# Gated-recurrence and softmax mixer: heads by pairs, four weight units held back into the softmax steps

## The reference, cut to what matters

```python
def _hybrid_mixer(h, w_in, conv_w, conv_b, gate_w, gate_b, lam, f_b, qk_g, w_out):
    u, gate, q, k, v, f = jnp.split(h @ w_in, ...)
    y_rnn = _rglru_branch(u, gate, ...)            # convolution, two gates, a scan over the tokens, gelu(gate)
    qh = _rmsnorm(_heads(q, 8), qk_g[0]); kh = _rmsnorm(_heads(k, 8), qk_g[1])
    logf = jax.nn.log_sigmoid(f + f_b)
    # softmax attention, 8 heads of 64, causal:
    # s = q.k * scale + c[query] - c[key],  c = cumsum(logf);  p = softmax(s);  y = p @ v
    return jnp.concatenate([y_rnn, y_fox], axis=-1) @ w_out
```

## Time and profile before

| | us |
|---|---|
| median of 3 runs | 2993.77 |
| the profiled execution | 2994.8 |
| its span, first to last instruction | 2993.1 |
| TensorE busy | 2903.7 (97%) |
| TensorE weight loads | 2344.5 (78%) |
| VectorE busy | 1471.6 (49%) |
| ScalarE busy | 1001.0 (33%) |
| mean granted TensorE clock | 0.988 of full speed |

### The profile page before, as it was taken

One profiled execution on the slowest core, in us unless ns is written; L12 is line 12 of the kernel. 1 busy time (PEld: TensorE's weight loads), 2 busy tenths in 40 slices (PEclk: granted clock), 3 DMA queues, 4 the chain that ended last, 5 costly groups with the idle time before them and its releaser, 6 DMA issues. The chain is left out here.

```text
span 2993.1 us, 33982 instructions
## 1 busy us (share of the span) xinstructions
PE 2903.7 (97%) x13410; PEld 2344.5 (78%) x13410; DVE 1471.6 (49%) x1906; ACT 1001.0 (33%) x1128; POOL 32.8 (1%) x66
## 2 busy tenths in 40 slices
PE   7999999999999999999999999999999989899998
PEld 5888887568888888888887888888866567688886
DVE  5764346446753476543544444436444843533333
ACT  4222227333222322223544322325432443232222
POOL 0000000000000000000000000000000000000000
PEclk9999999899999999999999999999999999999999
DMA  4432231014432343223111322234211112122221
GB/s 165 140 119 98 100 127 71 15 64 141 146 107 107 108 142 133 105 99 101 60 54 57 113 98 98 89 109 155 102 55 53 43 56 98 72 99 98 94 103 71
DMA packets 63742, 289.03 MB, mean 97 GB/s; under 512 B 9392, under 2 KB 26160, under 8 KB 33568
## 3 DMA queue, kind: packets, MB, share of 16 engines
q1 hardware_dynamic: 55072, 257.97, 24.3%
q0 software_dynamic: 8000, 29.50, 2.9%
q10 hardware_dynamic: 576, 0.23, 0.0%
HBM read 285.57 MB, written 2.10 MB: 96 GB/s over the span
## 5 line engine op out<-in xcount | busy, mean ns | idle before, releaser
L912 DVE TENSOR_TENSOR sb_WL<-sb_RAW,sb_WH 128x2048 fp32r<-128x2048 f32 x243 | 556.8, 2292 | 852.9 <-ACT sb_WH L403 852.9
L1602 PE MATMUL PS<-sb_HH,sb_WH 128*128 128x512 f32 x2352 | 934.2, 397 | 32.9 <-DVE sb_WL L912 24.2
L1603 PE MATMUL PS<-sb_HL,sb_WH 128*128 128x512 f32 x2352 | 920.1, 391 | 0.0
L1604 PE MATMUL PS<-sb_HH,sb_WL 128*128 128x512 f32 x2352 | 919.9, 391 | 0.0
L403 ACT ACTIVATE sb_WH<-sb_RAW 128x2048 fp32r<-128x2048 f32 x243 | 464.9, 1913 | 797.6 <-PE PS L1604 794.8
L1602 PEld LDWEIGHTS PS<-sb_HH,sb_WH 128*128 128x128 f32 x2352 | 444.8, 189 | 137.6 <-issue 38.6
L1603 PEld LDWEIGHTS PS<-sb_HL,sb_WH 128*128 128x128 f32 x2352 | 444.6, 189 | 95.2 <-issue 5.0
L1604 PEld LDWEIGHTS PS<-sb_HH,sb_WL 128*128 128x128 f32 x2352 | 444.2, 189 | 94.4
L1602 PE MATMUL PS<-ff_GH,sb_WH 128*128 128x512 f32 x880 | 342.4, 389 | 1.9 <-DVE sb_WL L912 1.9
L1604 PE MATMUL PS<-ff_GH,sb_WL 128*128 128x512 f32 x880 | 342.3, 389 | 0.0
L1603 PE MATMUL PS<-ff_GL,sb_WH 128*128 128x512 f32 x880 | 342.3, 389 | 0.0
(11 more groups left out here) (341 smaller groups left out, 2674.8 us busy)
## 6 DMA issues: line engine op xcount, KB each, us to landing
sb_RAW<-in_weights SPq DMA_DIRECT2D x233, 1024.0 KB, 4.8
ff_ADAW<-in_w_ada POOLq DMA_DIRECT2D x48, 512.0 KB, 4.0
sb_RAW<-in_weights SPq DMA_DIRECT2D x16, 512.0 KB, 4.9
sb_XT<-in_x SPq DMA_DIRECT2D x1, 2048.0 KB, 9.9
out_t<-sb_XT SPq DMA_DIRECT2D x4, 512.0 KB, 3.2
b_CT<-in_ctx POOLq DMA_DIRECT2D x1, 1024.0 KB, 5.4
sb_RAW<-in_weights SPq DMA_DIRECT2D x4, 256.0 KB, 4.1
hy_BD<-in_c_gates POOLq DMA_DIRECT2D x1, 512.0 KB, 3.5
```

The source lines that it names most:

```text
L912: dve.tensor_tensor(WL[slot][:, :], RAW[slot][:, :], f32(WH[slot][:, :]), ALU.subtract).then_inc(*T["w_lo"].up())
L1602: pe.matmul(out, wh, xh, start=start, stop=False)
L1603: pe.matmul(out, wh, xl, start=False, stop=False)
L1604: return pe.matmul(out, wl, xh, start=False, stop=stop)
```

## The change

The first mixer is laid out like the second one, with these parts:

1. Units: seven are run before the attention, in the order u, u, f, q0, k0, gate, gate (q0 and k0 hold the first four heads' pairs, two each). The second half of q and k, and all of v, are held back: q2 and k2 come in one slot from two half loads (`load_pair`), then v0, then q3 and k3, then v1. They are run as eight `part_step`s of half a unit, in bank 7.
2. Heads by pairs: for every row block, the q.k matmuls of both heads stand side by side, one on rows 0 to 63, one on rows 64 to 127. The order of the blocks is 2, 0, 1, 3, packed in three banks per head. A pair's `values` alternate likewise on the lower and the upper 64 output partitions of bank 6.
3. `CH` holds the high part of c in rows 0 to 7 and the low part in rows 32 to 39, and `SEL` has its selection rows twice, so one matmul adds both.
4. `turned(h)`: the ten transposes go back into the head's own score banks, one ScalarE copy of 1280 columns takes them out (`fox_pt`).
5. The normalisation of q and k is split into eight single steps (`squares`, `head_sum`, `root`, `normed`), the last four between the steps of the attention; the forget gate's chain is moved to the start. The recurrence (`recur`), its gelu and its product stand between softmax steps.
6. The first output group's matmuls (`first_out`) are put around the last pair's values; the other three groups are written out instead of looped, with banks (7,0), (4,5), (6,7), (4,5).

```diff
-HY_VISITS = ([("feat", (n, i)) for n in ("u", "q", "k", "gate") for i in range(2)] + [("gates", ("f", 0))]
-             + [("tok", ("v", i)) for i in range(2)])
+HY_VISITS = [("feat", ("u", 0)), ("feat", ("u", 1)), ("gates", ("f", 0)), ("feat", ("q", 0)), ("feat", ("k", 0)),
+             ("feat", ("gate", 0)), ("feat", ("gate", 1))]
+HY_UNITS = [0, 1, 8, 2, 4, 6, 7, (3, 5, 0), 9, (3, 5, 1), 10]
+HY_STEPS = [("q", 2), ("k", 2), ("v", 0), ("v", 1), ("q", 3), ("k", 3), ("v", 2), ("v", 3)]
+FOX_OFF = {3: 0, 2: 512, 0: 896, 1: 1024}
+FOX_ORDER = (2, 0, 1, 3)
```

ScalarE's program, from the first four gates on:

```diff
+            gate(0, hy["R"])
+            squares(2)
+            squares(3)
+            logs_table()
+            root(0)
+            root(1)
...
+            prepare(6)
+            root(2)
+            root(3)
...
+            gate(1, hy["I"])
...
+            prepare(7)
+            logs_table()
+            fox_exp(0)
+            fox_exp(1)
+            squares(4)
+            fox_pt(0)
+            fox_pt(1)
+            root(4)
...
+            squares(5)
+            prepare(8)
+            logs_table()
+            fox_exp(2)
+            fox_exp(3)
```

VectorE's program, from the first softmax step on:

```diff
+            fox_max(0)
+            fox_max(1)
+            recur(0)
+            fox_norm(0)
+            fox_norm(1)
+            take_part(0)
+            recur(1)
+            recur(2)
+            recur(3)
+            normed(4)
+            take_part(1)
+            prepare(8)
+            fox_max(2)
+            fox_max(3)
+            fox_norm(2)
+            fox_norm(3)
+            normed(5)
+            take_part(2)
```

TensorE's program:

```diff
+            def fox_scores(p):
+                pe.wait_ge(T["qk_norm"].sem, (3, 4, 6, 8)[p])
+                for i in FOX_ORDER:
+                    o, w = FOX_OFF[i], P * (i + 1)
+                    for h in (2 * p, 2 * p + 1):
+                        r = slice(64 * (h % 2), 64 * (h % 2) + 64)
+                        if p and i == FOX_ORDER[0]:
+                            pe.wait_ge(T["fx_pt"].sem, h - 1)
+                        pe.matmul(zs(h)[:, o:o + w], hy["Q"][r, p, P * i:w], hy["K"][r, p, 0:w], start=i != 0, stop=True, skip_group_check=True)
+                    for h in (2 * p, 2 * p + 1):
+                        pe.matmul(zs(h)[:, o + P * i:o + w], hy["EYE"][:, :], hy["MASK"][:, :], start=False, stop=True, skip_group_check=True)
+                        pe.matmul(zs(h)[:, o:o + w], hy["SEL"][:, h, :], hy["CH"][:, 0:w], start=False, stop=True, skip_group_check=True)\
+                            .then_inc(*T["fx_s"].up())
...
+            visit(0)
+            norm(N_NORM["mix0"])
+            visit(1)
+            visit(2)
+            pe.wait_ge(T["rms_ready"].sem, N_NORM["mix0"] + 1)
+            rms_columns(4)
+            visit(3)
+            visit(4)
...
             gates(0)
+            head_sum(0)
+            head_sum(1)
             visit(5)
+            head_sum(2)
+            head_sum(3)
             gates(1)
             visit(6)
...
             fox_scores(0)
+            part_step(0)
+            turned(0)
+            turned(1)
+            head_sum(4)
+            part_step(1)
+            fox_scores(1)
+            head_sum(5)
+            part_step(2)
+            part_step(3)
+            turned(2)
+            turned(3)
+            fox_values(0)
+            part_step(4)
+            fox_scores(2)
+            head_sum(6)
+            part_step(5)
+            fox_values(1)
+            turned(4)
+            turned(5)
+            head_sum(7)
+            part_step(6)
+            fox_scores(3)
+            part_step(7)
+            turned(6)
+            turned(7)
+            fox_values(2)
...
+            first_out(*hyo, 0, 0, 6)
+            first_out(*hyo, 0, 6, 7)
+            fox_values(3)
+            first_out(*hyo, 1, 0, 7)
+            first_out(*hyo, 0, 7, 8)
+            first_out(*hyo, 1, 7, 8).then_inc(*T["visit_done"].up())
+            residual(RES["hy"], U_HYO, (8,), HY_YH, HY_YL, False, g_from=1)
```

More of the change, by code:

```diff
@@ L261, in raw_need, with pairs_before @@
             return 16 * (u // 2 + 1) + (32 if u % 2 else -32) * (u >= U_SBO)
+        def pairs_before(u):
+            return sum(isinstance(unit, tuple) for unit in HY_UNITS[:u - U_HY + 1])
         def sb_raw(k):
@@ L315, in _ @@
                     load(s, 2 * i + s + 2)
[L316 to L317 removed]
+            for k, unit in enumerate(HY_UNITS):
+                sp.wait_ge(T["w_lo"].sem, U_HY + k - 1)
+                if isinstance(unit, tuple):
+                    load_pair((U_HY + k) % 2, (U_HY + unit[0], U_HY + unit[1]), unit[2])
+                else:
+                    load((U_HY + k) % 2, U_HY + unit)
+            with sp.Fori(0, (U_SB - U_HYO) // 2) as i:
+                for s in range(2):
+                    sp.wait_ge(T["w_lo"].sem, 2 * i + (U_HYO + s - 1))
+                    load((U_HYO + s) % 2, 2 * i + (U_HYO + s))
             for k, (kind, q) in enumerate(SB_LOADS):
@@ L583, in roots @@
[L583 to L595, removed]
+                    act.activation(dst[:, m, :], PS[:, 2 + m, :], ACT.Sigmoid, bias=col("gate_b", 4 * g + m)).then_inc(*T["rg_sig"].up())
@@ new lines, in _ @@
+            take(4)
+            prepare(5)
+            normed(0)
+            normed(1)
+            take(5)
+            prepare(6)
+            normed(2)
+            normed(3)
+            for m in range(4):
+                gain(m)
+            dve.wait_ge(T["xc_ready"].sem, 4)
+            for m in range(4):
+                dve.wait_ge(T["rg_sig"].sem, 4 + m + 1)
+                step(dve.tensor_tensor(I[:, m, :], I[:, m, :], XC[:, m, :], ALU.mult))
+            take(6)
+            prepare(7)
@@ new lines, in _ @@
+            for m in range(4):
+                dve.tensor_tensor(XC[:, m, :], XC[:, m, :], hy["GT"][:, m, :], ALU.mult).then_inc(*T["y_f32"].up())
+            take_part(3)
+            for m in range(4):
+                out_low(m + 1, HY_YH[m], HY_YL[m], XC[:, m, :])
+            prepare(9)
+            fox_low(0)
+            take_part(4)
+            fox_max(4)
+            fox_max(5)
+            fox_norm(4)
+            fox_norm(5)
+            normed(6)
+            take_part(5)
+            fox_low(1)
@@ L1276, in _ @@
+            prepare(10)
+            normed(7)
+            take_part(6)
+            fox_max(6)
+            fox_max(7)
+            fox_norm(6)
+            fox_norm(7)
+            take_part(7)
+            prepare(11)
+            fox_low(2)
+            fox_low(3)
+            residual(RES["hy"], U_HYO, 1, False, 1.0, "ffn1", ahead=U_HYO + 1)
             ffn(1)
@@ L1738, in _, with head_sum @@
-            for k in range(5):
-                if k == 2:
-                    pe.wait_ge(T["rms_ready"].sem, N_NORM["mix0"] + 1)
-                visit(k)
-                if k == 0:
-                    norm(N_NORM["mix0"])
+                    pe.matmul(PS[:, 2 + m, :], hy["BD"][:, 4 * g + m, :], hy["XC"][:, m, :], start=True, stop=True).then_inc(*T["rg_mm"].up())
+            def head_sum(i):
+                pe.wait_ge(T["qk_sq"].sem, i + 1)
+                if i >= 2:
+                    pe.wait_ge(T["qk_rms"].sem, i - 1)
+                pe.matmul(PS[:, i % 2 if i < 4 else 6, :], hy["B64"][:, :], SQT[:, i % 2, :], start=True, stop=True).then_inc(*T["qk_ss"].up())
```

446 lines of the change are left out of this document (211 added, 235 removed).

## The result

The changed kernel takes 2941.58 us (median of four runs, 2941.07 to 2943.32) where the kernel before took 2994.03 beside it (2993.01 to 2995.91): a ratio of 0.9825 [0.9808, 0.9842], 52 us less. The profiled execution is 2943.32 with a span of 2941.6.

A forecast was written before the change was run, and what follows sets the result against it. TensorE, busy 97% of the span, was taken to bound the kernel. Savings of 50.4 less 2.0 for extra changes and 1.1 for waits gave 47.3 off 2994.8, forecast 2947 us, range 2938 to 2961.

The forecast's parts named there:

- Stage and windows: First mixer, from 394 to the end of the fourth output unit: 223 instead of 270 us.
- Scores, 17.8: Attention scores: a pair of heads takes about 6.15 us against 10.60, saving 17.8 over four pairs.
- rival D: Array halves do not overlap with mask and c matmuls between blocks; 17.7 comes back, 2965; chance 3%.
- Values, 9.2: Attention values: four pairs at 2.3 us instead of eight heads, saving 9.2.
- Transposes, 8.5: Attention transposes: ten in a row take 1.3 us instead of 2.36 per head, saving 8.5.
- Clock and waits: Around the attention: low clock 8.0, waits 2.8 before first scores, 1.7 before output, 1.7 in heads, 0.7 idle, all saved.
- first head's waits: Attention: first and last head have 1.7 us more of waits than the steady ones, which go.
- Extra changes, -2.0: Around half units and single head sums: some ten more fp32/fp32r changes on TensorE at 0.2 each, costing 2.0 us.
- Waits, -1.1: New TensorE waits in the attention: 0.2 us at `head_sum(4)` and 0.9 at `part_step(3)`, costing 1.1.
- rival B: Softmax chain on the other engines replaces the old waits, 2.5 us late per pair: 2957; chance 24%.
- rival F: ScalarE table switches each take as long again as their load, 1.28 us more: 2953; chance 4%.
- Rival C and E: C: one long wait takes the clock down, 2958, 8%. E: finely cut stretch holds TensorE at low clock, 3052, 3%.

The follow-up runs named there:

- one_c: The kernel before with one c matmul per score block instead of two, low part of c in eight more rows: 3001.20 us, ratio 1.0006.
- rows_apart: The changed kernel with each head's mask and c matmuls directly behind its q.k, so the two heads' q.k are not side by side: 2977.35 us, ratio 0.9933.
- cols_apart: The changed kernel with a pair's values done one head after the other instead of alternating column halves: 2949.54 us, ratio 0.9840.
- idle_short: The changed kernel made to wait before the first scores for the high weights of the next unit, 2.3 us: 2948.68 us, ratio 0.9837.
- early_one_c: The kernel before with the forget gate's chain moved forward and one c matmul per score block: 2992.30 us, ratio 0.9979.
- early_c: The kernel before with the forget gate's chain moved forward, so TensorE does not wait for the low part of c: 2986.87 us, ratio 0.9964.
- plain_tail: The changed kernel with the last pair's values straight behind the third's and the whole output after them, not interleaved: 2946.47 us, ratio 0.9828.
- after_again: The changed kernel unedited, run again for comparison on another chip: 2942.24 us, ratio 0.9816.

## Why the prediction came out, step by step

- **Stage and windows.** Forecast 223 for the stage by windows against 270, measured 218.95 against 270.98. The mechanism and its places were right; the size was short by 4.7 of 52.0.
- **Scores, 17.8.** A pair takes 5.77, not 6.15, so 19.3. The four q.k blocks take 2.95, just as in my working; masks and c take 2.82 where I had twice 1.57. Two errors met there. A c matmul less brings 0.64 a head and not 0.79 (one_c), so a single head's masks and c are 1.72; but a pair's take 0.6 less than twice that, since what a block pays on entering them comes once for both heads (that this is the change of kind is my reading). That the row halves overlap is shown by rows_apart (12.0 to 14.2 more work), which also ends rival D.
- **Values, 9.2.** 2.31 a pair, as forecast, and by cols_apart their overlap is real. That experiment's price was mis-sized (6.15 in the stage, not 9.2): a serial pair with the new order is 3.85.
- **Transposes, 8.5.** 2.50, 2.27, 2.24 and 2.27 for the four pairs, 9.28 in all; the forecast had 10.4. 1.1 more gain.
- **Clock and waits, 8.0 + 2.8 + 1.7 + 1.7 + 0.7 = 14.9.** Measured before against after: clock 10.2 to 0 (my 8.0 was the two heads' scores only; the transposes behind them were slow too, and stood in my "first head's waits"). Forecast and measurement meet in the sum, not in each term: part of the 9.9 of idle time is the 0.37 waits that I had counted under transposes.
- **Extra changes, -2.0.** The term that was mis-sized most: by the stage there are none. All that is not scores, transposes, values or waits takes 176.1 after (218.95 less 23.06, 9.28, 9.21 and 1.25) and 176.3 before (270.98 less 91.26 for the heads and 3.45 of idle time ahead of them). A head sum and the half of v behind it show where the error lay: together 6.6 (503.20 to 509.81), where the durations that I used, 0.95 and 5.76, make 6.71. The change was in the head sum's 0.95 already, and I paid it twice.
- **Waits, -1.1.** 0.28 at `head_sum(4)` for 0.2, 0.97 at `part_step(3)` for 0.9, each behind the engine named. The first scores came at 476.93 for 477.7. So rival B (chains late by 2.5 a pair) fell by the trace, and walking the queues in order was worth it.
- **Sum.** 1.5 + 1.1 + 2.1 = 4.7, less 0.15 of waits: 4.6, against the 4.7 to be explained. All three errors lie on the same side, so the forecast came out 5 us too slow.
- **Table loads (rival F).** ScalarE after, a load and what stands around it:

```profile
493.74 0.63 ACT L462 ACTIVATE sb_HT<-sb_HT 128x512 f32<-128x512 f32 x1
494.39 1.28 ACT L683 ACT_TABLE_LOAD   x1
495.69 2.01 ACT L683 ACTIVATE hy_GT<-hy_GT 128x1024 f32<-128x1024 f32 x2
```

The load starts 0.02 after the instruction before it ends, and the gelu 0.02 after the load does. The Trainium skill (ScalarE: Activation LUTs, What ACT_TABLE_LOAD costs) has a drain of about 1.38 us beside each load; the trace does not agree, no such time is there.

- **Rival C and E.** No fall came, but they were nearer than I gave them. I had the clock follow waits alone. idle_short shows that 2.3 us were enough to cost 5.1 more, and rows_apart and early_one_c that unpaired scores with one c matmul lose it with no wait. What kept the clock at 1.00, given no wait, is by rows_apart the pairing that I had priced as 17.8 of work only: without it 35.7 come back, 21.5 to 23.9 of them clock. I was right on the clock for a reason that was not complete, and to that extent by luck.
- **What the parts are worth.** Against after: row pairing 35.7 of the stage, held-back projections 43.9, column pairing 6.2, interleaved output 4.5. Together that is 90.3, more than the 52.0: 42.7 of it is clock, which is lost when either of the first two is taken out, while the kernel before loses 10.2. The other parts of the change (`CH`'s low rows, the transposes in the score banks, the normalisation in single steps) were not taken out of the new kernel one by one.

## What to carry to other kernels

Pairing half-array matmuls pays twice, in work and in the clock that it keeps; look at both when you price it, and don't price an edit that takes full-array matmuls out of an otherwise unpaired stretch by its records alone (one_c: 5.1 less work, 0 less time). Walk the engines' programs in order with durations of rows: waits of 0.2 and 0.9 were forecast to a tenth of a microsecond, while the largest error came from a transition counted twice. When a stage shows "busy" and a low granted clock, check the matmuls before each fall as well as the waits.

## What the runs showed of the hardware that was not expected

- The clock falls to 1.2 GHz under a TensorE with no wait at all: rows_apart, some 22 to 24 us lost in four falls, each inside a pair's scores made head by head. Unpaired scores alone do not do it: with the second c matmul in each block they held 1.00 in early_c, with as many changes of kind in a head. Whether the clock answers to the 64 of 128 rows, or to the larger share of changes of kind, is open; no run here separates them.
- A wait of 2.3 us before the scores lowered it (idle_short), one of 3.11 before values did not (plain_tail). Nor is one place constant: the wait of 1.92 for weights in a later stage came with clock 1.00 in the kernel before, and with 0.89 after (windows below, before and then after). Which of them falls I can't say from these runs.

```profile
1922.00:1937.00 15.00, 13.08 (x58) 10.52 (x57) 6.58 (x7) 6.99 (x8) 0.00 (x0) 1.00 0.39 141
```

```profile
1870.00:1885.00 15.00, 13.08 (x51) 10.39 (x50) 6.17 (x6) 6.65 (x7) 0.00 (x0) 0.89 0.38 140
```

- The same kernel can fall or not: early_one_c's ten runs spread over 18 us on one chip, with granted clocks of 0.989 to 0.982 over the kernel, where after_again's five spread over 2.2, with 0.990 to 0.991.
